# Compressed attention of a one-layer decoder: its four chunks of queries in the order 2, 3, 1, 0 in place of 0, 1, 2, 3, with the first pair's masks made between its last steps

## The reference, cut to what matters

```python
s = jnp.einsum('bqghd,bngd->bghqn', qc, kc).astype(jnp.float32) * scale
dist = (t[:, None] - cmp_end[None, :]).astype(jnp.float32)
valid = cmp_end[None, :] <= t[:, None]
p_cmp = masked_softmax(s - sl * dist, valid) * jnp.any(valid, axis=-1)[:, None].astype(jnp.float32)
o_cmp = jnp.einsum('bghqn,bngd->bqghd', p_cmp.astype(dt), vc)
imp = jnp.einsum('bghqn,nm->bgqm', p_cmp, a_sel)
...
_, idx = lax.top_k(imp, k_sel)
```

## Time and profile before

| what | value |
| --- | --- |
| median of 3 runs | 3196.62 us |
| the three runs | 3193.91, 3196.62, 3683.84 us |
| profiled execution, its own time | 3190.18 us |
| its span, first to last instruction | 3188.1 us |
| PE busy | 2881.1 us, 90% of the span |
| DVE busy | 1423.9 us, 45% |
| mean granted clock of TensorE | 0.952 of full speed |
| compressed attention in it | 1006.8 to 1122.5 us, 3.6% of the span |
| first matmul of the sparse stage | 1125.5 us |

### The profile page before, as it was taken

How to read it: one execution, slowest core, us unless ns; L and a number is a source line. 1 busy time by engine, 2 the same in 40 slices (tenths; PEclk the granted TensorE clock), 3 DMA queues, 4 the chain that set the end, 5 groups by cost and what they waited for, 6 DMA issues and landing times. The chain is left out here.

```text
span 3188.1 us, 35846 instructions
## 1 busy us (share of the span) xinstructions
PE 2881.1 (90%) x12766; PEld 1663.3 (52%) x12767; DVE 1423.9 (45%) x3052; ACT 942.7 (30%) x1854; POOL 604.5 (19%) x588
## 2 busy tenths in 40 slices
PE   8999999999996689999989989999899799679990
PEld 4644444444445455666645556666544355456760
DVE  6621121221124856666656667888411222332227
ACT  0001000000002545555545546666411022113332
POOL 2111101101101511212130121000211333111116
PEclk9999999999998889999999989999999999789995
DMA  3211112112118101011010021010644344355848
GB/s 128 81 70 69 69 60 69 69 58 71 69 43 297 47 19 35 35 36 65 29 73 21 14 90 40 1 41 1 243 166 158 100 146 158 141 211 211 340 160 323
DMA packets 125916, 323.51 MB, mean 101 GB/s; under 512 B 13121, under 2 KB 53697, under 8 KB 117825
## 3 DMA queue, kind: packets, MB, share of 16 engines
q1 hardware_dynamic: 105744, 248.58, 22.1%
q0 software_dynamic: 13824, 50.34, 4.7%
q10 hardware_dynamic: 6192, 22.55, 1.7%
HBM read 206.41 MB, written 115.02 MB: 101 GB/s over the span
## 5 line engine op out<-in xcount | busy, mean ns | idle before, releaser
L389 PE MATMUL p_ps<-token_sums,p_ws 128*128 128x512 f32 x768 | 340.0, 592 | 0.0
L389 PEld LDWEIGHTS p_ps<-token_sums,p_ws 128*128 128x128 f32 x768 | 145.9, 190 | 183.7 <-issue 183.2
L417 DVE TENSOR_TENSOR p_kept<-p_ps,p_kept 128x512 f32<-128x512 f32 x96 | 66.5, 692 | 384.5 <-PE p_ps L389 384.5
L389 PE MATMUL p_ps<-xnT,p_w 128*128 128x512 f32 x512 | 232.2, 596 | 5.7 <-PEq L60 5.7
L1182 PE MATMUL b_po<-b_probT,vsw 128*64 128x256 f32 (+1 forms) x1824 | 232.4, 373 | 0.0
L1254 DVE CUSTOM_DVE_ANT_0 b_prob_s<-b_pq,b_sel 128x640 f32<-128x640 f32 (+5 forms) x192 | 168.6, 911 | 129.4 <-PE b_pq L1146 122.5
L399 ACT ACTIVATE p_kept<-p_ps 128x512 f32<-128x512 f32 x32 | 19.1, 597 | 667.5 <-PE p_ps L389 667.5
L1428 PE MATMUL d_pq<-d_keys,d_q 64*128 64x512 f32 (+3 forms) x640 | 187.2, 582 | 17.0 <-DMA d_keys<-projT 10.4
L1537 DVE CUSTOM_DVE_ANT_0 d_prob<-d_pq,d_bias 128x1024 f32<-128x1024 f32 (+6 forms) x192 | 168.0, 910 | 73.6 <-PE d_pq L1428 71.6
L417 DVE TENSOR_TENSOR p_stage<-p_ps,p_kept 128x512 f32<-128x512 f32 x128 | 88.2, 689 | 240.5 <-PE p_ps L389 240.5
L1206 ACT ACTIVATE b_prob_s<-b_prob_s,b_neg 128x1152 f32<-128x1152 f32 (+15 forms) x128 | 152.7, 1194 | 127.6 <-DVE b_neg L1262 127.5
(11 more groups left out here) (306 smaller groups left out, 4706.1 us busy)
## 6 DMA issues: line engine op xcount, KB each, us to landing
projT<-p_stage SPq DMA_DIRECT2D x128, 256.0 KB, 2.4
y<-e_y ACTq DMA_DIRECT2D x43, 512.0 KB, 4.3
p_w<-in_wt SPq DMA_DIRECT2D x16, 1024.0 KB, 5.3
gates_T<-projT SPq DMA_DIRECT2D x16, 1024.0 KB, 10.1
wgu<-in_w_gu SPq DMA_DIRECT2D x4, 4096.0 KB, 15.2
y<-m_zeros POOLq DMA_DIRECT2D x20, 512.0 KB, 20.1
p_xin<-in_x SPq DMA_DIRECT2D x16, 512.0 KB, 3.5
mergedT<-m_stage SPq DMA_DIRECT2D x8, 1024.0 KB, 11.6
```

The costliest lines, as they stand in the source:

```text
L389: mm = nc.tensor.matmul(ps[n % 8][:], weights[:, k, :], moving[:, k, :], start=(k == 0), stop=(k == HK - 1))
L417: nc.vector.tensor_tensor(out, bank[i], other, ALU.add).then_inc(summed, 1)
```

## The change

The chunks go in the order 2, 3, 1, 0. `place` gives a chunk's position in that order and takes the part of `c` wherever `c` counted turns: buffers, semaphores, the places of `turn`, `importance` and `choose`. SP loads the chunks in the new order. Since a later chunk is now narrower than an earlier one, `values` and `importance` contract only over the chunk's width. On POOL the four mask instructions stand behind `add_up(13)` and ahead of `add_up(14)` and `add_up(15)`; they wait for the first choice now (chunk 2 is first), where they waited for the third.

```diff
-            load_chunk(0)
+            load_chunk(CMP_ORDER[0])
             sp.dma_start(s.vsw[:], d["vsw"]).then_inc(vsw_in, 16)
-            load_chunk(1)
+            load_chunk(CMP_ORDER[1])
...
-            load_chunk(2)
-            load_chunk(3)
+            load_chunk(CMP_ORDER[2])
+            load_chunk(CMP_ORDER[3])
...
+CMP_ORDER = [2, 3, 1, 0]
...
-    steps = [(c, i) for c in range(NCH) for i in range(PAIRS)]
+    steps = [(c, i) for c in CMP_ORDER for i in range(PAIRS)]
+    place = {c: k for k, c in enumerate(CMP_ORDER)}
+    MASK_AT = 13
-    sel_turn = {PAIRS * c + 5: c for c in range(NCH)}
+    sel_turn = {PAIRS * place[c] + 5: c for c in CMP_ORDER}
...
+            def first_masks():
+                pool.wait_ge(s.b_dist_in[0], 64)
+                pool.wait_ge(chosen, place[2 * PAIR_ORDER[0] // 4] + 1)
+                for j in range(2):
+                    for g in range(GROUPS):
+                        mask_row(s, nc.gpsimd.tensor_tensor, 0, j, g).then_inc(s.b_first_masked, 1)
 
             pool.wait_ge(cleared, 4)
             for n in range(NS):
                 add_up(n)
-            pool.wait_ge(s.b_dist_in[0], 64)
-            pool.wait_ge(chosen, 2 * PAIR_ORDER[0] // 4 + 1)
-            for j in range(2):
-                for g in range(GROUPS):
-                    mask_row(s, nc.gpsimd.tensor_tensor, 0, j, g).then_inc(s.b_first_masked, 1)
+                if n == MASK_AT:
+                    first_masks()
...
-                    mm = nc.tensor.matmul(po[g * HD:(g + 1) * HD, :], s.vc[:, g * HD:(g + 1) * HD], probT[:, n % 2, g, :], start=True, stop=True)
+                    mm = nc.tensor.matmul(po[g * HD:(g + 1) * HD, :], s.vc[0:width(n), g * HD:(g + 1) * HD], probT[0:width(n), n % 2, g, :], start=True, stop=True)
...
-                        mm = nc.tensor.matmul(pi[:, g, j, :], sumT[:, g, j * P:(j + 1) * P], s.overlap[:], start=True, stop=True)
+                        mm = nc.tensor.matmul(pi[:, g, j, :], sumT[0:w, g, j * P:(j + 1) * P], s.overlap[0:w, :], start=True, stop=True)
```

More of the change, by code:

```diff
@@ L592, in compressed_attention @@
     AX = mybir.AxisListType
-    steps = [(c, i) for c in range(NCH) for i in range(PAIRS)]
+    steps = [(c, i) for c in CMP_ORDER for i in range(PAIRS)]
+    place = {c: k for k, c in enumerate(CMP_ORDER)}
     NS = len(steps)
     LAST = NS + 4
+    MASK_AT = 13
     slopes = [2.0 ** (-8.0 * (h + 1) / N_ALIBI) for h in range(NSA_HEADS)]
-    sel_turn = {PAIRS * c + 5: c for c in range(NCH)}
-    sel_product = {PAIRS * c + 6: c for c in range(NCH)}
-    sel_choice = {PAIRS * c + 7: c for c in range(NCH)}
+    sel_turn = {PAIRS * place[c] + 5: c for c in CMP_ORDER}
+    sel_product = {PAIRS * place[c] + 6: c for c in CMP_ORDER}
+    sel_choice = {PAIRS * place[c] + 7: c for c in CMP_ORDER}
     step_use, sum_use, uses = {}, {}, 0
@@ L654, in add_up @@
                 rate = stat[:, n % 4, 3].unsqueeze(3).to_broadcast([P, GROUPS, 4, w])
-                acc = pbar[c % 2][:, :, :, 0:w]
+                acc = pbar[place[c] % 2][:, :, :, 0:w]
                 pool.wait_ge(rate_ready, n + 1)
                 if i == 0:
-                    if c >= 2:
-                        pool.wait_ge(turned, sum_use[c - 2] + 1)
+                    if place[c] >= 2:
+                        pool.wait_ge(turned, sum_use[CMP_ORDER[place[c] - 2]] + 1)
                     nc.gpsimd.tensor_tensor(acc, prob[n % 4][:, :, :, 0:w], rate, ALU.mult).then_inc(summed, 1)
@@ L730, in _ @@
                     c = sel_turn[n]
-                    pe.wait_ge(summed, PAIRS * c + PAIRS)
-                    turn(pbar[c % 2], sum_use[c])
+                    pe.wait_ge(summed, PAIRS * place[c] + PAIRS)
+                    turn(pbar[place[c] % 2], sum_use[c])
                 if n in sel_product:
@@ L777, in _ @@
                     c = sel_turn[n]
-                    copy(sumT, sum_use[c], weights_at[c - 1] if c >= 1 else 0)
+                    copy(sumT, sum_use[c], weights_at[CMP_ORDER[place[c] - 1]] if place[c] >= 1 else 0)
                 if n + 2 < NS:
@@ L831, in choose @@
                 dve.wait_ge(valued, weights_at[c])
-                if c == 0:
+                if place[c] == 0:
                     dve.wait_ge(s.select_in, 32)
-                if c >= 1:
-                    dve.wait_ge(chosen, c)
+                else:
+                    dve.wait_ge(chosen, place[c])
                 whole = [P, GROUPS, 4, NBLK]
                 nc.vector.tensor_tensor(imp[:], pi[:], s.keep[:, ts, :].unsqueeze(1).to_broadcast(whole), ALU.mult).then_inc(weighed, 1)
-                dve.wait_ge(weighed, c + 1)
+                dve.wait_ge(weighed, place[c] + 1)
                 link(nc.vector.tensor_tensor(imp[:], imp[:], s.force[:, ts, :].unsqueeze(1).to_broadcast(whole), ALU.add))
```

9 lines of the change are left out of this document (5 added, 4 removed).

## The result

The changed kernel takes 3208.9 us (median of six runs, 3203.1 to 3213.0), the kernel before 3195.6 us in runs on the same chip. The ratio is 1.0046, with a 95% interval of 1.0035 to 1.0057: 13 us slower where 3195 was forecast and 3205 was the end of the range. By the bound of 2% it is the same; by its own interval it is slower.

A forecast was written before the change was run, and what follows sets the result against it. Only 116 us, 3.6% of the span, was open to the change, with the wide chunks bound by DVE. Six terms, 1.9 - 6.4 + 4 + 4.5 - 2.7 - 1.2, summed to +0.1 us: 3195 us, range 3186 to 3205.

The forecast's parts named there:

- Term 1: Start of the stage: the first rate comes later because the first chunk is wider; plus 1.9 us, between 1.5 and 2.5.
- Term 2: Between steps 4 and 5: ACT's wait for step 0's store goes; minus 6.4 us, down to minus 3.4.
- Term 3: Narrow chunks 1 and 0 directly behind a choice wait for PE at low clock; plus 4 us, 0 to plus 6.
- Term 4: Masks on POOL beside the gates, mainly `gate(14)`, make DVE instructions wait; plus 4.5 us, 0 to plus 9.
- term 5: Tail of the stage: without masks beside them, two DVE instructions get shorter; minus 2.7 us.
- Term 6: Last gate of the stage: it is now narrow, so two of its instructions get shorter; minus 1.2 us.
- The whole chain: Rival: DVE's chain stays whole, PE waits do not return, masks slip into DVE's waits; sum -7, 3188 us; chance 0.20.
- The slower end: Rival: every mask stops DVE in `gate(14)` and `gate(15)` on the path; sum +5.6 or more, 3201 us; chance 0.13.
- The store's hole: Rival: step 0's store lands later by what it is issued later, so the wait stays; +3, 3198 us; chance 0.07.
- the sparse stage started at 0.50 of its clock: Rival on the next stage: PE's changed idle time moves the full clock's return, 5 us either way, 3190 or 3200; chance 0.07.
- The test that I had named: The prediction would be wrong if the store's wait stayed, or the stage ended outside 1114 to 1132 us.

The follow-up runs named there:

- e3: Changed kernel plus extra matmuls: 10 ahead of the turns of steps 3 to 7, 26 ahead of steps 8 and 12; 1.0018 of the time before.
- e12: Changed kernel with values and importance contracting over all 128 rows again, leftover rows not cleared, masks still behind step 13; 1.0005 of the time before.
- e1: Changed kernel with the four masks behind the sums of all 16 steps; 1.0035 of the time before.
- e13: Changed kernel with both products over all 128 rows, leftover rows not cleared, and masks behind the last sum; 0.9989 of the time before.
- e10: Changed kernel's code in the old chunk order 0, 1, 2, 3, masks last, both products still over fewer rows; 1.0027 of the time before.
- e15: Changed kernel's code in the order 0, 1, 2, 3, masks last, both products over all 128 rows; 1.0002 of the time before.
- e4: Kernel before with the next stage's loads issued one by one behind the stores of steps 1 to 11; 0.9986 of the time before.
- e16: Changed kernel with masks last, both products over all 128 rows, and POOL clearing the columns a wider chunk left; 0.9992 of the time before.
- e11: Changed kernel with masks last and 26 extra matmuls ahead of the turns of steps 8 and 12 only; 1.0018 of the time before.
- e8: Changed kernel's code in chunk order 0, 2, 1, 3, masks last, next stage's loads spread behind the stores; 1.0005 of the time before.
- e2: Changed kernel with the four masks behind the sum of step 7; 1.0035 of the time before.
- e5: Changed kernel with masks last and extra matmuls ahead of the turns of steps 3 to 8 and 12; 0.9993 of the time before.

## Why the prediction was wrong

The step that failed is the sentence on the rows: "The contraction over fewer rows changes neither the number of matmuls nor their columns. No row shows one over 32 or 96 rows; I take it as 0, between minus and plus a fifth of the 1.08 us that four of them take now". The instruction itself is as long as I said: at full clock four products over 32 rows took 1.07 us (e3, at 1097.91), at low clock four over 64 took 1.97. The Trainium skill, TensorE: Matmul & The Clock Gate, says in the table of "Why this matters for your kernels" that a single matmul over 32 rows takes the time of one over 128; these numbers agree. What fewer rows changed was which of the two clocks the stage got, and the bound that I set held the price of one instruction, not of all behind it. It measured 13.0 us of stage (122.3 - 109.3, changed against e12), 15.1 with masks last (e1 against e13), 10.3 in the old order (e10 against e15); by the medians, each beside its own runs of before, 12.5, 13.3 and 7.5 us.

The rest of the sum, point by point:

- Term 1, plus 1.9: the first rate came 1014.38 - 1012.51 = 1.87 us later.
- Term 2, minus 6.4: ACT's copy out of step 2 waited for no store, and the rate of step 4 stood at 1038.31 us, forecast near 1038. In the old order the same hole, taken away by the spread loads (e4), was worth 4.9 us of stage.
- Term 3, plus 4: with the rows given back nothing speaks against it, though no run takes it by itself. A low round cost 5.97 - 4.03 = 1.94 us in chunk 1 of e13 (forecast 1.8) and 5.91 - 2.94 = 2.97 in chunk 0 (forecast 2.9). In e13, without masks beside the gates, the stage is 106.7 - 109.9 = -3.3 us, and -1.4 with the later first rate. The terms without the masks say 1.9 - 6.4 + 4 - 1.2 = -1.7. With fewer rows the assumption behind it, one low round for each chunk and full clock otherwise, did not hold: from 1070 us on there were no rounds at full clock.
- Term 4 with term 5, plus 4.5 and minus 2.7, so plus 1.8: e12 against e13 is 109.3 - 106.7 = +2.6 us. The mechanism is in the rows above, 1.93 and 2.01 us where the instructions alone took 0.17, in two of the four named and not in all. `gate(14)`'s rate came 10.30 us after that of step 13, in e13 5.91 us. But where PE is the late engine (changed against e1) the masks cost 0.6 us of stage. The Trainium skill, SBUF — State Buffer, "Who interferes with whom", cited in the prediction, held here too: of the instructions in that gate the reduction took its 0.41 us.
- Term 6 is in the rows, and no run takes it apart from the others.

With all 128 rows the forecast would have stood: 3195.1 us measured in e12, 1.0005 of the time before, forecast 3195. The stage's end there is plus 1.2 us with the start, the sum said plus 0.1. e12 does not clear the extra rows; e16, which does, has the masks last, and there the clears cost 0.2 us against e13. So the sum was right for a kernel that differs from the changed one in the number of rows.

None of the rivals came about in the changed kernel. The whole chain had 3188 us. The slower end had 3201, nearer to the 3208.9 measured, but by another mechanism: `gate(14)` ended 11.2 us after the rate of step 13 (12 had been named), and without the masks beside it (e1) the stage is 0.6 us shorter. The store's hole was gone, and the sparse stage started at 0.50 of its clock for 26 us (1137 to 1163 us), as before. The test that I had named, a stage that ends outside 1114 to 1132 us, was right to say that the prediction would then be wrong.

Still open: why fewer rows keep the clock low. The runs show only that it stays low for long with 32 and 64 rows in the values, that it does not with 128 rows of zeros, and that with extra matmuls over 128 rows ahead of two turns (e11, the traced execution) it stays high through the same narrow products. In the changed kernel chunk 2, with 96 rows, shows no difference to e12 (0.63 against 0.69 from 1008 to 1021 us, 0.74 against 0.68 from 1021 to 1035). In e8, where chunk 2 stands behind chunk 0, the clock was 0.50 from 1021 to 1035 us with PE busy 14.00 of 14.00 us, but the products in that window were still those of chunk 0, over 32 rows; it came back with the first one over 96:

```profile
1037.85 1.97 PE L718 MATMUL a_po<-a_probT,vc 32*64 32x512 f32 x4
...
1041.71 1.97 PE L710 MATMUL a_pt<-ident,a_gated 128*128 128x128 f32 x8
1043.61 1.21 PE L718 MATMUL a_po<-a_probT,vc 96*64 96x512 f32 x4
```

Nor do few rows hold the clock down without fail. In e10 it came back at 1059.95 us, in a product over 64 rows, after 46 us at 0.50; in e8 a product over 64 rows at 1077.86 took 1.14 us, right behind a turn of 1.97.

```profile
1059.95 1.07 PE L715 MATMUL a_po<-a_probT,vc 64*64 64x512 f32 x4
```

Some 6.6 of the 20.9 us between the two profiled spans lie behind the stage. The medians differ by 13.3 us and do not ask for them: the profiled execution of before was 5.4 us below its median, that of after 2.2 above.

## What to carry to other kernels

Cutting the rows of a product to what is needed saved no time in the product itself here, and it kept TensorE at its low clock for tens of microseconds, which cost 13 us of a stage of 110. Before trusting a sum that takes an edit at nothing because each instruction keeps its length, look at which stretches run at which clock and whether TensorE could become the late engine at the low one. When a change of order disappoints, put the new code back in the old order: that one kernel (e10) pointed at the cause where four variations of the suspected ones (e1, e2, e3, e5) had not, and giving the rows back (e12, e13, e15) confirmed it. A window's clock is read together with the instructions that are really in it: in PE's list the values of a step stand three steps behind the scores.
